# One-hot products written side by side, four staging buffers for the gate table, and three normalisations with root and reciprocal on 8 or 16 columns

## The reference, cut to what matters

```python
# group A (SSD): mean square over 128 channels, two groups
yg = y.reshape(b, s, SSM_GROUPS, di // SSM_GROUPS)
yg = yg * lax.rsqrt(jnp.mean(yg * yg, axis=-1, keepdims=True) + NORM_EPS)
# group C (RWKV-7): length of kk over 64 channels of a head, before the scan
kk = kk / jnp.maximum(jnp.sqrt(jnp.sum(kk * kk, axis=-1, keepdims=True)), 1e-12)
# group C, after the scan: group norm over 64 channels of a head
mean = jnp.mean(y, axis=-1, keepdims=True)
var = jnp.mean((y - mean) ** 2, axis=-1, keepdims=True)
y = ((y - mean) * lax.rsqrt(var + RWKV_GN_EPS)).reshape(b, s, g_) * ln_w + ln_b
y = y + (jnp.sum(r * k * r_k, axis=-1, keepdims=True) * v).reshape(b, s, g_)
# PEER: 512 tokens, 8 heads, 16 picks each out of 128 x 128 experts of width 1024
act = jax.nn.gelu(jnp.einsum('td,tkd->tk', xb, u[ib]))
return jnp.einsum('tk,tkd->td', gb * act, v[ib])
```

## Time and profile before

| | us |
|---|---|
| median of 3 timed runs | 3776.54 |
| their lowest and highest | 3772.18, 3790.19 |
| the profiled execution | 3758.81 |
| its span, first to last instruction | 3757.1 |
| PE busy | 3213.4 (86%) |
| DVE busy | 2486.8 (66%) |
| ACT busy | 855.0 (23%) |
| moved by DMA | 943.33 MB, mean 251 GB/s |

### The profile page before, as it was taken

The page is one execution under the profiler, slowest core; times in us unless marked ns, Lnnn a source line. Parts: engine busy times, 40 slices in busy tenths (PEclk is TensorE's granted clock), DMA queues, the critical chain, the costliest instruction groups (busy, mean ns, idle before and its releaser), DMA issues. The chain is left out here.

```text
span 3757.1 us, 39887 instructions
## 1 busy us (share of the span) xinstructions
PE 3213.4 (86%) x13220; PEld 2251.4 (60%) x13220; DVE 2486.8 (66%) x5256; ACT 855.0 (23%) x2022; POOL 887.8 (24%) x856
## 2 busy tenths in 40 slices
PE   7949877598799999999688489785987999999995
PEld 6727666475466666666266267574754666666662
DVE  4675556887686666666646764569877766666666
ACT  2433312157300000000023333121573000000000
POOL 0012202226422222222100232032363222222221
PEclk9969878899899999999899798787998999999997
DMA  3100113279999999999731001033799999999997
GB/s 116 46 0 1 56 39 97 95 236 367 346 408 417 417 417 416 416 417 405 309 105 34 1 36 37 23 107 126 242 356 351 414 417 417 416 416 416 416 403 291
DMA packets 235344, 943.33 MB, mean 251 GB/s; under 512 B 19584, under 2 KB 85632, under 8 KB 164864
## 3 DMA queue, kind: packets, MB, share of 16 engines
q0 software_dynamic: 73728, 536.90, 35.2%
q1 hardware_dynamic: 95360, 370.31, 25.9%
q10 hardware_dynamic: 66048, 33.56, 3.1%
HBM read 904.52 MB, written 35.65 MB: 250 GB/s over the span
## 5 line engine op out<-in xcount | busy, mean ns | idle before, releaser
L1926 PE MATMUL bank<-peer_x_late,xT 128*128 128x256 f32 x4096 | 938.2, 383 | 93.1 <-ACT peer_acts_u L1992 49.9
L2054 DVE CUSTOM_DVE_ANT_0 peer_slots<-peer_slots,wide 128x1024 f32<-128x1024 f32 x512 | 628.6, 1228 | 514.9 <-DMA peer_slots<-in_peer_uv,peer_rows 512.4
L1926 PEld LDWEIGHTS bank<-peer_x_late,xT 128*128 128x128 f32 x4096 | 786.4, 192 | 303.5 <-issue 152.2
L1874 POOL DMA_INDIRECT peer_slots<-in_peer_uv,peer_rows x512 | 518.1, 1012 | 1462.5 <-DVE h L2065 1317.3
L1946 PE MATMUL bank<-ring,peer_acts_u 128*128 128x512 f32 x1280 | 585.2, 602 | 50.4 <-DVE peer_acts_u L2085 34.5
L2065 DVE SCALAR_TENSOR_TENSOR h<-peer_slots,peer_coef,h 128x1024 f32<-128x1024 f32 x416 | 533.6, 1283 | 8.0 <-DVE peer_coef L2062 0.6
L1946 PEld LDWEIGHTS bank<-ring,peer_acts_u 128*128 128x128 f32 x1280 | 246.0, 193 | 307.5 <-issue 296.2
L1946 PE MATMUL bank<-ring,wide 128*128 128x512 f32 x768 | 346.9, 597 | 6.5 <-DMA ring<-in_peer_uv 6.4
L1946 PEld LDWEIGHTS bank<-ring,wide 128*128 128x128 f32 x768 | 146.8, 192 | 159.2 <-issue 146.6
L1992 ACT ACTIVATE peer_acts_u<-bank 128x256 f32<-128x256 f32 x160 | 60.2, 380 | 671.2 <-PE bank L1926 662.8
L2046 DVE TENSOR_TENSOR peer_hot<-iota,peer_picks 128x512 f32<-128x512 f32 x256 | 167.1, 699 | 61.9 <-PE bank L1915 51.5
(11 more groups left out here) (459 smaller groups left out, 4198.2 us busy)
## 6 DMA issues: line engine op xcount, KB each, us to landing
xT<-in_peer_ut SPq DMA_DIRECT2D x256, 512.0 KB
ring<-in_peer_uv SPq DMA_DIRECT2D x256, 512.0 KB
gates<-peer_staging ACTq DMA_DIRECT2D x32, 1024.0 KB
peer_staging<-gates SPq DMA_DIRECT2D x32, 1024.0 KB, 18.9
ring<-in_w_in SPq DMA_DIRECT2D x48, 512.0 KB, 3.6
ring<-in_peer_wq SPq DMA_DIRECT2D x32, 512.0 KB, 3.6
nsa_w<-in_cmp_w SPq DMA_DIRECT2D x2, 4096.0 KB, 12.2
ring<-in_w_out SPq DMA_DIRECT2D x16, 512.0 KB, 4.4
```

What stands on the lines that cost most here:

```text
L1874: nc.gpsimd.indirect_dma_start(out=p.slots[:, n % ROW_SLOTS, :], out_offset=None, in_=A["peer_uv"], in_offset=bass.IndirectOffsetOnAxis(ap ...
L1926: last = nc.tensor.matmul(k.bank[bank_of[j]][:, 0:DENSE], u_raw[:, j % U_RING, b * P:(b + 1) * P], p.x_late[:, b, :], start=b == 0, stop=b ...
L2054: nc.vector.tensor_tensor_reduce(out=u, in0=u, in1=k.wide[:, t, :], scale=1.0, scalar=0.0, op0=ALU.mult, op1=ALU.add, accum_out=p.dots[:, ...
```

## The change

It has three parts.

1. In each of the three normalisations PE now puts tokens on the partitions: the block of squares is the stationary operand and a column of ones (SSD) or two columns of the block matrix `same[64]` (RWKV) the moving one, so that the sums are 128x8 or 128x16. DVE and ACT do the constant, the root and the reciprocal on these. A second set of products, with a column of the result broadcast as the stationary operand and `ident` as the moving one, writes them 128x512 again into PSUM, and DVE multiplies from there. In the operand stage the small constant stands ahead of the scans. In the group norm two instructions are merged into others (`scalar_tensor_tensor`).
2. The four products of a quad are written element by element side by side (a stride of 4 elements in the bank), and the copy reads the bank in order and writes runs of 4 elements.
3. There are four staging buffers; the two new ones lie in `k.ring`. So the first four tiles of v are loaded after the 21 first tiles of u and after the last store from their buffer.

```diff
@@ ssd_mixer
-                for g in range(2):
-                    act.wait_ge(s["norm_var"], g + 1)
-                    nc.scalar.activation(k.xT[:, 2 + g, :], k.xT[:, 2 + g, :], ACT.Sqrt).then_inc(s["norm_dev"], 1)
+                act.wait_ge(s["norm_var"], 1)
+                nc.scalar.activation(k.stat[:, 8:16], k.stat[:, 0:8], ACT.Sqrt).then_inc(s["norm_dev"], 1)
...
+                dve.wait_ge(s["norm_sum"], 2)
+                nc.vector.tensor_scalar(k.stat[:, 0:8], k.bank[0][:, 0:8], 1.0 / P, EPS, ALU.mult, ALU.add).then_inc(s["norm_var"], 1)
+                dve.wait_ge(s["norm_dev"], 1)
+                nc.vector.reciprocal(k.stat[:, 16:24], k.stat[:, 8:16]).then_inc(s["norm_inv"], 1)
                 for g in range(2):
...
-                    step(nc.vector.reciprocal(k.xT[:, 2 + g, :], k.xT[:, 2 + g, :]))
+                    dve.wait_ge(s["norm_wide"], g + 1)
...
-                                                        in1=k.xT[:, 2 + g, :], op0=ALU.mult, op1=ALU.mult))
+                                                        in1=k.bank[1 + g][:, :], op0=ALU.mult, op1=ALU.mult))
...
-                    nc.tensor.matmul(k.bank[g][:, :], k.ones[:, :], k.xT[:, g, :], start=True, stop=True).then_inc(s["norm_sum"], 1)
+                    for t in range(TT):
+                        last = nc.tensor.matmul(k.bank[0][:, g * TT + t:g * TT + t + 1], k.xT[:, g, t * P:(t + 1) * P], k.ones[:, 0:1],
+                                                start=True, stop=True)
+                    last.then_inc(s["norm_sum"], 1)
+                pe.wait_ge(s["norm_inv"], 1)
+                for g in range(2):
+                    for t in range(TT):
+                        at = 16 + g * TT + t
+                        last = nc.tensor.matmul(k.bank[1 + g][:, t * P:(t + 1) * P], k.stat[:, at:at + 1].to_broadcast([P, P]), k.ident[:, :],
+                                                start=True, stop=True)
+                    last.then_inc(s["norm_wide"], 1)
@@ operand stage of RWKV (kk), DVE
-            dve.wait_ge(s["kk_ready"], 2)
+            dve.wait_ge(s["kk_sum"], 1)
+            nc.vector.tensor_scalar(k.dt[:, :], k.bank[6][:, 0:4 * TT], 1e-30, None, ALU.max).then_inc(s["kk_var"], 1)
             dve.wait_ge(s["gates"], 4)
...
+            dve.wait_ge(s["kk_dev"], 1)
+            step(nc.vector.tensor_scalar(k.dt[:, :], k.dt[:, :], 1e-12, None, ALU.max))
+            nc.vector.reciprocal(k.dt[:, :], k.dt[:, :]).then_inc(s["kk_inv"], 1)
             step(nc.vector.tensor_tensor(mix[:, 2:4, :], mix[:, 2:4, :], bonus, ALU.mult))
...
-            step(nc.vector.reciprocal(tmp, tmp))
-            step(nc.vector.tensor_tensor(kk, kk, tmp, ALU.mult))
...
+                dve.wait_ge(s["kk_wide"], i + 1)
+                step(nc.vector.tensor_tensor(kk[:, i, :], kk[:, i, :], k.bank[6 + i][:, :], ALU.mult))
@@ carry_and_compressed, DVE
+                dve.wait_ge(s["root"], 1)
+                nc.vector.reciprocal(k.stat[:, 0:4 * TT], k.stat[:, 16:16 + 4 * TT]).then_inc(s["inverse"], 1)
                 dve.wait_ge(s["summed"], 1)
                 for i in range(2):
                     step(nc.vector.tensor_tensor(k.mixed[:, 6 + i, :], k.mixed[:, 6 + i, :], k.bank[6 + i][:, :], ALU.add))
-                dve.wait_ge(s["root"], 1)
-                step(nc.vector.reciprocal(sq, sq))
-                step(nc.vector.tensor_tensor(dev, dev, sq, ALU.mult))
...
@@ experts
             def load_v(j):
                 if j >= V_RING:
                     sp.wait_ge(s["v_done"], j - V_RING + 1)
+                else:
+                    sp.wait_ge(stored[2 + j // 2], 16 * (GROUPS // STAGES))
...
-                if 0 <= j - (RUN_AHEAD - V_RING) < V_RING:
-                    load_v(j - (RUN_AHEAD - V_RING))
-            for g in range(2):
-                sp.wait_ge(stored[g], 16 * (GROUPS // 2))
+            for j in range(V_RING):
+                load_v(j)
+            for n in range(STAGES):
+                sp.wait_ge(stored[n], 16 * (GROUPS // STAGES))
             load_gates(0)
...
-                    last = nc.tensor.matmul(k.bank[2 + q % 2][:, n * P:(n + 1) * P], p.hot2[:, at, :], p.hot1[:, at, :],
+                    last = nc.tensor.matmul(k.bank[2 + q % 2][:, :].rearrange("p (j t) -> p t j", t=4)[:, n, :], p.hot2[:, at, :], p.hot1[:, at, :],
...
-                if q % 4 == 0 and g >= 2:
-                    act.wait_ge(stored[g % 2], 16 * (g // 2))
+                if q % 4 == 0 and g >= STAGES:
+                    act.wait_ge(stored[stage_of(g)], 16 * (g // STAGES))
                 at = 4 * (q % 4)
-                nc.scalar.copy(spread[:, g % 2, :, at:at + 4].rearrange("p j t -> p t j"),
-                               k.bank[2 + q % 2][:, :].rearrange("p (t j) -> p t j", t=4)).then_inc(s["copied"], 1)
+                nc.scalar.copy(spread_of(g)[:, :, at:at + 4],
+                               k.bank[2 + q % 2][:, :].rearrange("p (j t) -> p j t", t=4)).then_inc(s["copied"], 1)
```

More of the change, by code:

```diff
@@ L834, in _ @@
             for i in range(2):
-                nc.tensor.matmul(k.bank[6 + i][:, :], k.same[64][:, :], tmp[:, i, :], start=True, stop=True).then_inc(s["kk_sum"], 1)
+                for t in range(TT):
+                    at = 2 * (i * TT + t)
+                    last = nc.tensor.matmul(k.bank[6][:, at:at + 2], tmp[:, i, t * P:(t + 1) * P],
+                                            k.same[64][:, :].rearrange("p (e c) -> p e c", e=2)[:, :, 0], start=True, stop=True)
+            last.then_inc(s["kk_sum"], 1)
+            pe.wait_ge(s["kk_inv"], 1)
+            for i in range(2):
+                for t in range(TT):
+                    at = 2 * (i * TT + t)
+                    for e in range(2):
+                        last = nc.tensor.matmul(k.bank[6 + i][64 * e:64 * e + 64, t * P:(t + 1) * P], k.dt[:, at + e:at + e + 1].to_broadcast([P, 64]),
+                                                k.ident[:, :], start=True, stop=True)
+                last.then_inc(s["kk_wide"], 1)
             pe.wait_ge(s["rk_ready"], 2)
@@ L1412, in _ @@
                     nc.scalar.activation(sq[:, i, :], dev[:, i, :], ACT.Square).then_inc(s["squares"], 1)
-                act.wait_ge(s["var_ready"], 2)
-                nc.scalar.activation(sq, sq, ACT.Sqrt).then_inc(s["root"], 1)
+                act.wait_ge(s["var_ready"], 1)
+                nc.scalar.activation(k.stat[:, 16:16 + 4 * TT], k.stat[:, 0:4 * TT], ACT.Sqrt).then_inc(s["root"], 1)
             @block.tensor
@@ L1462, in _ @@
                     pe.wait_ge(s["squares"], i + 1)
-                    nc.tensor.matmul(k.bank[i][:, :], k.same[64][:, :], sq[:, i, :], start=True, stop=True).then_inc(s["var_sum"], 1)
+                    for t in range(TT):
+                        at = 2 * (i * TT + t)
+                        last = nc.tensor.matmul(k.bank[0][:, at:at + 2], sq[:, i, t * P:(t + 1) * P],
+                                                k.same[64][:, :].rearrange("p (e c) -> p e c", e=2)[:, :, 0], start=True, stop=True)
+                last.then_inc(s["var_sum"], 1)
+                pe.wait_ge(s["inverse"], 1)
+                for i in range(2):
+                    for t in range(TT):
+                        at = 2 * (i * TT + t)
+                        for e in range(2):
+                            last = nc.tensor.matmul(k.bank[2 + i][64 * e:64 * e + 64, t * P:(t + 1) * P], k.stat[:, at + e:at + e + 1].to_broadcast([P, 64]),
+                                                    k.ident[:, :], start=True, stop=True)
+                    last.then_inc(s["var_wide"], 1)
 def nsa_mixer(nc, k, r, A, l):
@@ L1567 @@
 READ = 8
+STAGES = 4
 CHOOSE_AT = {2: 0, 3: 12, 1: 82}
@@ L1815, in experts @@
         v_in = [s[f"v_in{n}"] for n in range(V_RING)]
[L1816 removed]
+        g_in, stored = (s["g_in0"], s["g_in1"]), [s[f"stored{n}"] for n in range(STAGES)]
         u_raw = k.xT[:, :, :].rearrange("p b t -> p (b t)").rearrange("p (n c) -> p n c", n=U_RING)
[L1818 removed]
+        halves = p.staging[:, :].rearrange("p (g j t) -> p g j t", g=2, j=P)
+        ring_halves = k.ring[:, :, :].rearrange("p u c -> p (u c)").rearrange("p (g j t) -> p g j t", g=2, j=P)
         near = p.staging[:, :].rearrange("p (e g j t) -> p e g j t", e=2, g=GROUPS, j=READ)
```

43 lines of the change are left out of this document (20 added, 23 removed).

## The result

The changed kernel takes **3731.21 us** (median of 4 runs, 3727.43 to 3737.73). The kernel before took 3775.31 us on the same chip (4 runs, 3772.18 to 3790.19). The ratio is 0.9885, with a 95% interval of 0.9862 to 0.9907: 44 us faster. Forecast were 3746.5 us in a range of 3718 to 3775.

What follows compares the result with a forecast made beforehand. The prediction took DMA as full in PEER and the mixers as one chain through the engines; 26 us from normalisations and 4 from the gate table off the 3776.5 us median gave 3746.5 us, range 3718 to 3775.

Steps and rivals of the forecast that it cites:

- SSD, 5.4 us: SSD stage's end: narrow sums and small steps replace two long reciprocals; gain 5.4 us, 3.3 if the clock is down.
- kk, 0.4 us: Operand stage: DVE's wait for PE's sums takes most of the gain; 0.4 us a layer, bounds -1 to 2.9.
- Group norm, 7.2 us: Group norm: narrow sums, second set mostly hidden behind DVE's add; gain 7.2 us, 5.3 at the lower clock.
- Sum of the normalisations, 26 us: Mixers: 5.4 + 7.2 + 0.4 = 13.0 us gained per layer, 26 us for two layers.
- The copy, 0.6 us: PEER's gate table: ACT's copy falls from 1.03 to 0.6 us, counting only as far as DMA has room.
- The late loads of v, +5.4 us a layer: PEER: v's first four loads, 2.1 MB, now lie ahead of the table's load, costing 5.4 us at 387 GB/s.
- The gate table, -2 us a layer: PEER's quads and table load: -7.4 + 5.4 = -2 us a layer, within +3.2 to -11.6.
- What is full is DMA.: PEER's stretch with the quads, 838:981: no engine is full, DMA is, with share 1.01 at 367 GB/s.
- With four buffers ACT may be four stores ahead ... the queue behind them is longer.: End of PEER's quads: quads end before 981, but DVE's and PE's wait ahead of the table gets longer.
- Rival A: PEER's quads: DMA is not the wall, ACT's waits and copies are; 31 us more gain, 3715 us; chance 12%.
- Rival B: PEER's quads: the strided write slows PE; at twice the product time 3818 us, slower than before; chance 10%.
- Rival C: Mixers and gate table: low clocks and waits leave only 9 us of gain in all, 3768 us; chance 16%.

Runs made afterwards that it cites:

- Experiment 6: Changed kernel with unread products on PE, 8 ahead of SSD's sums and 3 ahead of its second set: 3731.33 us.
- Experiment 5: Changed kernel with gate stores issued by SP: 3724.01 us; with kk's constant behind the scans: 3729.23 us; with both: 3711.37 us.
- experiment 3: Kernel before with side-by-side layout, two buffers: 3766.03 us; the same with v late: 3782.53 us. Changed kernel with the old layout: 3731.57 us.
- both edits: Changed kernel with gate stores issued by SP instead of ACT and kk's constant behind the scans: 3711.37 us, ratio 0.9827 to the kernel before.
- experiment 4: Changed kernel storing only a sixteenth of each group of gates, the table's loads taking as many bytes from another matrix: 3661.24 us.

## Why the prediction was right, and where not

The direction and the range held; the number was 15 us too high. By the steps of the prediction:

- **SSD, 5.4 us: measured 3.6.** Sums and small steps came nearly as computed: the second set began at 210.59, in a stage that ran 0.27 us ahead of the old one, so 0.2 us behind the forecast 210.65. But the set was given 2.1 us and took 3.78. I had named the low clock as the lower bound (3.3) and taken the upper one. Experiment 6 shows that the clock made it so. In the same text I took the low clock for kk "since PE has been idle"; ahead of SSD's second set PE is idle as well.
- **kk, 0.4 us: measured 0.7** (34.37 us from the stage's start to L816, before 35.04 to L809). The mechanism came as told: sums in 2.74 us (I took 2.6), the second set in 3.31 at a granted clock of 0.60 in 247:251 (I took 3.9), DVE waiting in front of its scans, everything behind them later. Experiment 5 takes that wait away and gains 3.4 us, close to the 3.8 by which the prediction had the scans late. PE's sums start at 235.59 and are done at 238.33, the scans could start at 234.7, and nothing of kk is wanted before the exponentials are out.
- **Group norm, 7.2 us: measured 7.1.** From 502.32 to 497.97 it starts 4.35 us sooner, and it ends 11.48 sooner. The second set took the 1.97 us of its model in the earlier trace rows, at a granted clock of 1.00. PE had been idle 0.80 us right ahead of it, much as in SSD (0.74). What differs is the time before: PE was busy 8.00 of 8 us from 490 to 498 here, and 0.81 of 3 us from 205 to 208 in SSD.
- **Sum of the normalisations, 26 us: 22 by the profiles, 24 by the runs.**
- **The copy, 0.6 us: measured 0.57.** That it counts only as far as DMA has room held better than I used it: with four buffers it shows no gain at all (experiment 3).
- **The late loads of v, +5.4 us a layer: 6.2 and 10.9 in the profiles, 8 by the medians, 6 by the means, 4 by the ratios.** The term is right in sign, and in size as far as these tell.
- **The gate table, -2 us a layer: measured -7.4** (15 us for two layers), inside the bounds of +3.2 to -11.6. **This is the step that failed**, in its size. The gain ahead of v's loads was put at 7.4 us, from 367 GB/s in 838:981 up to the 387 of six microseconds; with v's 5.4 us it came to 12.8. The base was too high: in 838:981 the second profile of before has 338 GB/s. By the same working that would be 18.1 - 5.4 = 12.7 us less a layer, and the measured 7.4 lies between. The changed kernel's own 382 GB/s needed no more than 387. But as what DMA does when it is full, 387 was wrong too: the quads' stretch ran at 396 GB/s with the stores by SP, and with both edits at 403 (shown next). The two buffers were worth 9 to 12 us a layer (experiment 3). The signs looked like the forecast's all the same, which is luck of the first profile: against S the last store left 7.4 us sooner (5 to 15 forecast) and the table's load 1.4 us (2 forecast).

The same stretch with both edits:

```profile
828.00:963.00 135.00, 118.03 (x547) 73.53 (x545) 113.37 (x217) 88.37 (x274) 98.58 (x76) 0.99 1.05 403
```

- **"What is full is DMA."** Half right. The transfers set the pace (experiment 4), but in two of three profiles of the old gate table DMA had room among the quads: shares 0.92 and 0.91, at 332 and 328 GB/s. I read a single profile, and it stood 17.7 us under the median, as the prediction noted. I shifted the sum by these 17.7 us, as though the change left them alone. By the other two profiles they lie in PEER, from S to E, where the change acts: a part of this loss goes away with the new gate table. Which part isn't shown, since one profile has it before L and the other behind.
- **"With four buffers ACT may be four stores ahead ... the queue behind them is longer."** It came so, and went one step further than I thought: the issue of a store can hold its engine, 18.8 us in one place. Four buffers aren't needed for that: with two and v late the last stores stand 13.9 and 14.1 us, with two and v early 0.5. So the late loads of v beside the last stores have a part in it. Ahead of the table DVE waits 13.6 us, forecast "well over 13", before 13.3; PE waits 25.4, before 19.5.
- **Rival A** (DMA is not the wall, 3715) falls as a mechanism: fewer bytes stored gave 70 us, and a shorter copy none that shows. Its number leaves the forecast's own 4 us for the table in the sum; by its terms it is 3776.5 - 26 - 31 = 3719. The measured 3731 stands between it and the forecast, so the time alone would not have told them apart. What it had right is that there was room in DMA.
- **Rival B** (the strided write slows PE, 3818) falls: 290 ns on average for a record of L1960 (first layer), against 297 in the first and 299 in the second profile of before, and 289 in experiment 3 with the stride undone; the shortest and the median, 272 and 275, are the same in all four. The Trainium skill ("PSUM — Partial Sum Buffer", Specifications) says that any non-contiguous pattern slows matmuls significantly. No row here agrees; for these float32 products the price is under the difference between two profiles.
- **Rival C** (clocks and waits eat it, 3768): SSD's clock is its part that came true, 1.7 of the 1.8 us that SSD fell short in a layer. Group norm, kk and table didn't.

## What to carry to other kernels

Compare the profile with the spread of the runs before taking bounds from it: where it is quick, find out in which stretch, since a second profile of the same kernel may differ in just the part that the change acts on, and a third may put the difference elsewhere. A DMA share near 1 doesn't say that the rate is at its ceiling, so look for the same mix of transfers at a higher rate. When more buffers let an engine run ahead, give the issue of the transfers to a queue behind which no compute waits. A wait for a small sum belongs behind the work that doesn't need it, and a short set of products behind a stretch in which PE was mostly idle is to be priced at the lower clock.

## What the runs showed of the hardware

- Issuing a transfer can hold its engine. Stores of 1 MB took 0.52 us of ACT at least and in most cases; in the first profile after others took 2 to 5 us, and the last of each layer 18.8 and 16.4. In the second profile after these two took 3.6 and 12.9, and with two buffers and late loads of v 13.9 and 14.1. On SP the longest took 19.4 us. What limit is reached isn't shown.
- Two executions of the kernel before differ by 8 and 11 us in a stretch of 200 us with many queues at work, and by under 3 us in all other parts. At 828:963 the rate was 356 GB/s in one and 332 in the other, with no instruction different. A third, of the same gate table, differs from them by 4 to 8 us in the part behind.
- With 4 floats in a row per write, a copy of 512 columns took 567 ns; with single floats scattered, 1030 ns.
- Eight products of 128 columns took 3.78 us at a granted clock of 0.50, and 2.65 us at 0.82 after PE had been kept at work.
